# Convolution norms, the sample's softmax, its value pages and half of the even output projection woven into the 32 steps of the prompt attention

## The reference, cut to what matters

```python
z = h @ w_in_even                    # q, k, v, forget gates, a, b
o_fox = fox_attend(q, k, v, logf)    # prompt: causal softmax; sample: 8 pages of 128 keys/values
u = a * sigmoid(b)
cv = depthwise_conv(concat(state, u), width 31) + conv_b
cv = silu(group_norm(cv, 8) * g + b)
out = concat([o_fox, cv]) @ w_out_even     # 512 + 512 features in, 1024 out
x = x + g1 * out
# prompt attention, per head: s = q k^T / 8 + cum_q - cum_k, masked, softmax, p @ v
# sample attention, per sample: the same over cache_k, cache_v[page_table] (1024 rows) and its own row
```

## Time and profile before

| | us |
|---|---|
| median of 3 runs | 1930.45 (1929.25 to 1932.46) |
| profiled execution | 1925.21 |
| its span | 1923.4 |
| TensorE busy / VectorE / ScalarE / GpSimd | 1774.2 / 864.9 / 573.5 / 213.7 |

### The profile page before, as it was taken

How to read it: one execution, slowest core, us unless ns; L and a number is a source line. 1 busy time by engine, 2 the same in 40 slices (tenths; PEclk the granted TensorE clock), 3 DMA queues, 4 the chain that set the end, 5 groups by cost and what they waited for, 6 DMA issues and landing times.

```text
span 1923.4 us, 31960 instructions
## 1 busy us (share of the span) xinstructions
PE 1774.2 (92%) x12929; PEld 1549.1 (81%) x12929; DVE 864.9 (45%) x1461; ACT 573.5 (30%) x816; POOL 213.7 (11%) x229
## 2 busy tenths in 40 slices
PE   5899888779899999999899999999968799999997
PEld 3899443327799999999797879799738799999997
DVE  2699346613533232334634637337463533333324
ACT  2422443201442122122333434314331432222223
POOL 1000048600200000000100101101120100000001
PEclk7899668789999999999999999999978999999998
DMA  8463045577434434443231725334742123233321
GB/s 300 139 214 102 2 138 153 175 256 236 147 94 164 149 103 146 144 139 97 66 105 53 224 76 185 121 91 135 263 141 86 58 88 99 77 97 97 89 72 53
DMA packets 288066, 248.82 MB, mean 129 GB/s; under 512 B 9000, under 2 KB 239816, under 8 KB 287951
## 3 DMA queue, kind: packets, MB, share of 16 engines
q1 hardware_dynamic: 262740, 173.97, 29.8%
q0 software_dynamic: 15824, 58.99, 8.6%
q10 hardware_dynamic: 9395, 14.36, 2.1%
HBM read 224.05 MB, written 23.70 MB: 129 GB/s over the span
## 4 chain that ended last, share of the span: by engine, by line
PE 83%; DVE 6%; ACT 3%; POOL 3%; DMA 2%; issue 2%; ACTq 1%; SPq 0%; POOLq 0%; DVEq 0%
PE product L728 60%; PE product L743 5%; PE job L1140 2%; POOL sqa L2094 2%; DMA vp<-in_cache_v 2%; PE job L625 2%; PE job L619 1%; PE job L1123 1%; PE job L917 1%; PE job L658 1%; PE job L893 1%; PE job L1026 1%; PE job L1115 1%; DVE rstd L1591 1%; PE job L1046 1%
## 5 line engine op out<-in xcount | busy, mean ns | idle before, releaser
L728 PE MATMUL product<-H_hi,w_lo 128*128 128x260 f32 x2368 | 674.1, 285 | 3.0 <-ACT gate L1172 2.9
L728 PE MATMUL product<-H_lo,w_hi 128*128 128x260 f32 x2368 | 668.9, 282 | 0.0
L728 PE MATMUL product<-H_hi,w_hi 128*128 128x260 f32 x2368 | 668.4, 282 | 0.0
L728 PEld LDWEIGHTS product<-H_hi,w_lo 128*128 128x128 f32 x2368 | 445.5, 188 | 16.2 <-issue 14.2
L728 PEld LDWEIGHTS product<-H_hi,w_hi 128*128 128x128 f32 x2368 | 446.1, 188 | 0.0
L728 PEld LDWEIGHTS product<-H_lo,w_hi 128*128 128x128 f32 x2368 | 445.9, 188 | 0.2
L1561 DVE TENSOR_TENSOR w_lo<-raw,w_hi 128x1024 fp32r<-128x1024 f32 (+1 forms) x228 | 274.9, 1207 | 169.1 <-ACT w_hi L1172 168.2
L1172 ACT ACTIVATE w_hi<-raw 128x1024 fp32r<-128x1024 f32 (+1 forms) x228 | 234.6, 1037 | 308.2 <-PE product L728 188.9
L728 PE MATMUL product<-G_hi,w_lo 128*128 128x260 f32 x912 | 260.4, 286 | 5.9 <-DVE X L1645 2.5
L728 PE MATMUL product<-G_lo,w_hi 128*128 128x260 f32 x912 | 259.3, 284 | 0.0
L728 PE MATMUL product<-G_hi,w_hi 128*128 128x260 f32 x912 | 259.2, 284 | 0.0
(11 more groups left out here) (319 smaller groups left out, 2139.3 us busy)
## 6 DMA issues: line engine op xcount, KB each, us to landing
spare<-in_ada_w POOLq DMA_DIRECT2D x24, 1024.0 KB, 9.0
raw<-in_w_in_odd SPq DMA_DIRECT2D x48, 512.0 KB, 3.7
raw<-in_w_ffn_gate SPq DMA_DIRECT2D x44, 512.0 KB, 3.8
raw<-in_w_ffn_up SPq DMA_DIRECT2D x44, 512.0 KB, 3.6
kp<-in_cache_k SPq DMA_DIRECT2D x64, 256.0 KB, 2.7
raw<-in_w_ffn_down SPq DMA_DIRECT2D x32, 512.0 KB, 3.3
st<-in_state_ret POOLq DMA_DIRECT2D x28, 512.0 KB, 4.3
out_ret_sample<-st POOLq DMA_DIRECT2D x28, 512.0 KB, 4.5
```

What stands on the lines that cost most here:

```text
L728: mm = pe.matmul(Gp[slot][:, c, 0:CH], w[:, j, k, :], x[:, k, cols], start=k == 0 and p == 0, stop=k == kt - 1 and p == 2)
```

## The change

Stages 2, 4 and 5 and half of 6 lose their places. Their pieces are put into the steps x of the attention (and a few into the input blocks), each engine's code and the list of PSUM jobs following the same tables:

```diff
+QB_AT = {1: 2, 3: 3, 5: 4, 7: 5, 9: 6, 11: 7}
+VN_AT = {0: (0,), 1: (1,), 2: (2, 3)}
+KN_AT = {6: 0, 8: 1, 10: 2, 12: 3}
+VS_AT, KS_AT, LT_AT, CUM_AT = 4, 14, 3, 5
+CM_AT = {6: 0, 7: 1, 8: 2, 9: 3}
+CQ_AT, ROOT_AT, SILU_AT = 11, 12, 17
+CB_AT = {13: 0, 14: 1, 15: 2, 16: 3}
+PREP_AT = {11: 0, 21: 1}
+MT_AT = {12: 0, 22: 1}
+MB_AT = {13: 0, 23: 1}
+EXP_AT = {14: 0, 24: 1}
+DN_AT = {15: 0, 25: 1}
+V_AT = {17: 0, 19: 1, 21: 2, 23: 3, 27: 4, 29: 5, 31: 6}
+GATHER_AT = {18: 0, 20: 1, 22: 2, 24: 3, 28: 4, 30: 5}
+V_LOAD_AT = {5: (0, 1), 12: (2,), 18: (3, 4), 20: (5, 6), 22: (7, 8), 24: (9, 10), 28: (11, 12), 30: (13, 14)}
+CONV_OUT_AT = {19 + i: i for i in range(8)}
+PER_STEP = 3
+def pages_of(x):
+    return range(min(PER_STEP * x, NPG), min(PER_STEP * x + PER_STEP, NPG))
```

In the input blocks (TensorE; ScalarE and VectorE follow, with the samples' taps at m = 8 to 11 and the log forget values at 10 and 12):

```diff
+                elif m == 9:
+                    conv_rows()
+                elif m == 14:
+                    sums_of_forget()
+                elif m == 15:
+                    rows_of("qs", QT)
+                elif m == 17:
+                    turn_sums()
```

The centring is one product with identity minus mean; ScalarE copies and squares it from PSUM. The group rows are spread by 16 products of half height:

```diff
+            def group_rstd(t):
+                pe.wait_ge(conv_act, 1)
+                for c in range(2):
+                    bank = open_job(("cb", t, c))
+                    for e in range(2):
+                        mm = pe.matmul(bank[HD * e:HD * e + HD, 0:CH],
+                                       con[0:8, C_ID + 2 * t + e:C_ID + 2 * t + e + 1].broadcast_to((8, HD)),
+                                       CR[:, c * CH:(c + 1) * CH], start=True, stop=True)
+                    close(mm)
```

The samples' softmax is made for samples 0 to 3 and 4 to 7 apart. Values go in units of four pages, two units a sample, through three buffers; pages 0 and 1 of a unit are issued by SP, 2 and 3 by ScalarE:

```diff
+        def value_unit(eng, u, js):
+            if u < 2:
+                eng.wait_ge(block_done, N_OUT_EVEN)
+                eng.wait_ge(lo_ready, N_OUT_EVEN)
+            elif u == 2:
+                wait_job(eng, ("cq", 1))
+            elif u % 2 == 0:
+                wait_job(eng, ("ov", (u - 3) // 2))
+            else:
+                eng.wait_ge(v_used, (u - 3) // 2 + 1)
+            for j in js:
+                page(eng, 4 * u + j, cache_v, value_page(u, j), v_unit[u % 3])
...
+            def past_values(b):
+                bank = open_job(("ov", b))
+                pe.wait_ge(samp_dve, 7 + 5 * (b // 4))
+                for u in (2 * b, 2 * b + 1):
+                    pe.wait_ge(v_unit[u % 3], 64 * (u // 3 + 1))
+                    for j in range(4):
+                        mm = pe.matmul(bank[QD * j:QD * j + QD, :], weights_of(b, u % 2 * 4 + j), value_page(u, j),
+                                       start=u % 2 == 0, stop=u % 2 == 1)
+                    if u % 2 == 0:
+                        mm.then_inc(v_used, 1)
+                close(mm)
```

ScalarE copies each sample's bank into vm (before, VectorE multiplied it), and `gather` (`og`) picks the heads by two columns. The output projection becomes 16 blocks of 4 tiles: the convolution's half in steps 19 to 26, with its own update of X, and the attention's half behind the last gather:

```diff
+            def conv_out(i):
+                n = N_OUT_EVEN + i
+                if i == 0:
+                    pe.wait_ge(g_ready, 4)
+                pe.wait_ge(lo_ready, n + 1)
+                slots_free(0, conv_base + i - 1)
+                product(n % 4, n % 2, 4, G_hi[:, 4:8], G_lo[:, 4:8]).then_inc(block_done, 1)
...
+            gather(NB - 2)
+            past_values(NB - 1)
+            gather(NB - 1)
             pe.wait_ge(g_ready, 5)
-            wait_emptied(pe, ("o", HEADS - 1))
-            run("out_even", N_OUT_EVEN, 2, KD, G_hi, G_lo, "D")
+            run("out_even", N_OUT_EVEN + KD, 2, 4, G_hi, G_lo, "D")
```

On ScalarE, four gates, their roundings and two weight splits stand in step 17, and value units in the steps of V_LOAD_AT:

```diff
+                    if x == SILU_AT:
+                        conv_gates()
+                        ahead(N_OUT_EVEN)
+                        ahead(N_OUT_EVEN + 1)
+                    if x in CONV_OUT_AT:
+                        ahead(N_OUT_EVEN + CONV_OUT_AT[x] + 2)
+                    for u in V_LOAD_AT.get(x, ()):
+                        if u == 0:
+                            act.wait_ge(pages_loaded, 32)
+                        value_unit(act, u, (2, 3))
```

On VectorE, behind the dots of a step come the pieces of that step:

```diff
+                    if x == LT_AT + 1:
+                        past_logs()
+                    if x == CUM_AT:
+                        past_sums()
+                    if x in PREP_AT:
+                        past_prepare(PREP_AT[x])
+                    if x == CQ_AT:
+                        group_var()
+                    if x in CB_AT:
+                        group_scale(CB_AT[x])
...
+                    if x == SILU_AT + 1:
+                        for t in range(4):
+                            dve.wait_ge(ghi_ready, t + 1)
+                            n.up(minus_hi(G_lo[:, 4 + t, :], CV[:, t, :], G_hi[:, 4 + t, :]), g_ready)
+                        lo(N_OUT_EVEN)
+                        lo(N_OUT_EVEN + 1)
+                    if x in CONV_OUT_AT:
+                        i = CONV_OUT_AT[x]
+                        lo(N_OUT_EVEN + i + 2)
+                        update(i, N_OUT_EVEN + i, mod_at(0, 2))
```

SP's queue, in order (before: all key pages, four weight blocks, half of the value pages, four weight blocks):

```diff
+            key_pages(0, 4)
+            out_weights(N, N + 4)
+            key_pages(4, 20)
+            values(0, 2)
+            key_pages(20, 36)
+            values(2, 3)
+            key_pages(36, 52)
+            values(3, 5)
+            key_pages(52, 60)
+            values(5, 7)
+            out_weights(N + 4, N + 6)
+            key_pages(60, 64)
+            values(7, 9)
+            out_weights(N + 6, N + 8)
+            values(9, 11)
+            out_weights(N + 8, N + 12)
+            values(11, 16)
+            out_weights(N + 12, N + 16)
```

828 lines of the change are left out of this document (479 added, 349 removed).

## The result

The changed kernel takes 1904.0 us (median of 4 runs, 1900.3 to 1907.5), the kernel before, run beside it, 1930.9: ratio 0.986, interval 0.984 to 0.988. That is 27 us gained where I had forecast 61, and just outside my range. The profiled execution took 1902.9 us with a span of 1901.1.

A forecast was written before the change was run, and what follows sets the result against it. The attention's 32 steps were taken as paced by 64 GpSimd products of 1.27 us, TensorE close behind at clock 0.72. Start 54.5, steps and tail -18, projection 24.5: 61 us gained, profiled 1864, median 1869; range 1840 to 1903.

The forecast's parts named there:

- Start: Stages between input blocks and attention leave the path; GpSimd's first division at 209.3 us, 54.5 earlier.
- Steps 0 to 10: First woven attention steps, three GpSimd products each: GpSimd 47 us, TensorE 48 at full clock, taken as 57 us.
- TensorE needs 28 + 20 = 48 at full clock: In steps 0 to 10, TensorE's products take 48 us if its clock is 1.00.
- Steps 11 to 16: Step 11 with VectorE's 3.4 us reciprocal 11.5 us, the five others 28.5 together: 40 us.
- 17 and 18: Steps with ScalarE's gates, roundings, table loads, weight splits and page issues, and a late key page 52: 18 us.
- the sync queue puts value units ahead of key page 52, some 7 us, beside the same stall: In steps 17 and 18, key page 52 comes some 7 us late, alongside the stall for ScalarE's gates.
- Steps 19 to 26: TensorE's own work, half blocks, values and gathers: 57 us at full clock plus 2 for waits, 59 us.
- Tail: From step 27 until the second projection can start, value pages wait for three buffers: 28.5 us.
- Behind G ready: From the second projection's start to the next norm: half the products and weights' low parts made before, 24.5 us gained.
- the rival that gives 1919: TensorE's clock stays at 0.73 in woven steps and tail, 253 us instead of 202.5; chance 0.10.
- a clock under 0.7 in the woven steps: Sign of being wrong: TensorE's granted clock below 0.7 in the attention steps that carry the added work.
- Queues lock: Rival: four banks shared in one order by all jobs cost 1 us more a step, 32 us, giving 1901; chance 0.20.

The follow-up runs named there:

- split sums: VectorE's seven running additions cut into 2, 3 and 2 over steps 4 to 6, page sums in step 7, against a kernel of 1870.6 us: 1870.5 us.
- the undo: Against keys first, the eight woven half blocks of the convolution's projection run behind the attention instead: 1902.4 us, ratio 0.9859 against 0.9782.
- keys first: Against the changed kernel, the sync queue issues key pages 36 to 63 before the value units they stood behind: 1886.7 us, ratio 0.9782.

## Why the prediction was wrong

The mechanism was the one forecast and its sign was right; five terms of the sum were too small. At the norm the forecast was 437 and the trace has 472.0: 35 us.

*Start*, 209.3 forecast, 213.0 measured (209.5 to 213.4 over all runs). Right to 4 us.

*Steps 0 to 10*, 57 forecast, 61.9 measured, 66 in most other runs. The term is 5 to 10 us too small. The pages aren't the cause (66.8 us without them). The step that failed is "TensorE needs 28 + 20 = 48 at full clock": the attention before had 0.72, and the changed kernel got 0.78 here and has TensorE busy for 55.0 us. In the runs of 66 to 67 us it had 0.68 to 0.73 and was busy for 60 to 63; in the two of 73 and 77 us it had 0.59 and was busy for 70 and 73. The 48 over the clock are 61.5 us at 0.78 and 66 to 71 at 0.73 to 0.68, an estimate from these rows that fits, and 81 at 0.59, which is too much. So the steps lasted about as long as TensorE took at the clock it got. No run changed the clock alone, so this is how the runs go together and not an experiment, and what sets the clock in these steps stays open.

A smaller term was mis-sized too. I took VectorE's seven running additions from a stretch where GpSimd did nothing, 274 ns each. In step 4 GpSimd makes products beside them. The view by tile, of the changed kernel and then of the run with split sums, has their shortest, median and longest:

```profile
L1967 DVE TENSOR_TENSOR EX<-EX,LT x7: 274/275/1222, 240.2 to 243.8; 128x64 f32<-128x64 f32 x7
```

```profile
L1984 DVE TENSOR_TENSOR EX<-EX,LT x7: 266/1224/1232, 242.7 to 256.5; 128x64 f32<-128x64 f32 x7
```

An addition takes 274 ns, or 1.04 to 1.23 us where it meets a product of GpSimd, which takes 1.27. In the change two of the seven met one, and that made them 1.7 us longer (3.85 in all); cut into three pieces six of them did, 7.45 in all. That is 3.6 of the 5.6 us by which steps 0 to 10 are longer there at most, since TensorE's clock fell to 0.59 in the same run. The Trainium skill ("SBUF — State Buffer", Who interferes with whom) has this as a rule: a VectorE instruction with two SBUF inputs contends with a GpSimd instruction that reads SBUF, and the ports that they share are an exclusive lock. Both traces agree with it. I hadn't priced it.

*Steps 11 to 16*, 40 against 47.1, and *17 and 18*, 18 against 21.5. Here the step "the sync queue puts value units ahead of key page 52, some 7 us, beside the same stall" failed, twice over. It isn't beside: with the order mended the steps take 39.7 and 15.6 us. And I had seen one such place where there are three: units 2, 3 and 4, and 5 and 6. The wait before page 36, 9.7 us, had no term at all, although the order was in the diff. Of the 10.5 us by which the two terms were small, the queue's order accounts for all: with it mended the two are 13.3 us shorter. It isn't the clock that gave this in steps 11 to 16, since 6.3 of the 7.4 us there are idle time of TensorE that went (11.1 to 4.8).

The Trainium skill ("ScalarE: Activation LUTs", What ACT_TABLE_LOAD costs) has 2.66 us for a change of set, by which I had the sum 3 to 5 us longer. The trace doesn't bear it out. Step 17 of the changed kernel has a load of 1.28 us, and ScalarE's next instruction begins 0.02 us behind it:

```profile
327.51 1.28 ACT L1317 ACT_TABLE_LOAD   x1
328.81 2.95 ACT L1317 ACTIVATE CV<-CV,vec 128x520 f32<-128x520 f32 x4
```

*Steps 19 to 26*, 59 forecast and 58.7 measured, right by two errors: GpSimd waited 9.3 us in them for page 60, and with the order mended they are 5.1 us shorter; the work itself takes 52 to 54, less than the 57 that I had at the full clock. My term took the half blocks as 23.6 us on top of the rest; the undo shows that they cost these steps 8.3.

*Tail*, 28.5 against 37.9. I had priced the release of a buffer to the landing of its pages at 5.5 to 6 us and counted three waits. That step was too small: two more buffers alone took 8.6 us off, without pages the tail is 25.3, with room for every unit 25.4 to 27.1. I hadn't counted two things that the trace shows. ScalarE issues pages in front of its own copies, 3.7 us in steps 28 and 30 each, and the last unit behind the head's copy; but with two more buffers the tail is 29.3 and 29.5 us with these issues and 29.1 without, so they aren't shown to cost anything there by themselves. And the clock was 0.72, at which the output of the last head took 3.9 us instead of 3.0; in the short tails it is 0.79 to 0.93, and how much of their gain is the clock's isn't separated.

*Behind G ready*, 25.4 against 32.0. "The weights' low parts are made before" and the loads were right; what failed is that I took the norm's own chain as before, hidden below a block of 5.9 us. A block of 2.95 us is shorter than ScalarE's split and square and GpSimd's 1.5 us addition, so the chain came out from under it. Woven in, the stage takes 23.7 to 25.7.

*The clock.* Over the woven steps and the tail it was 0.77 (the stretches above, by their length), near the 0.73 of the rival that gives 1919. I had named a clock under 0.7 in the woven steps as a sign of being wrong, and steps 11 to 18 had 0.65 and 0.66. The rival fails as a whole, for it has TensorE at work all the time, and it was busy for 182 of the 227 us up to G ready; without pages steps 11 to 18 ran at 0.72 and 0.73 and took what I had forecast for a full clock. But it is half right: steps 0 to 10 went with the clock, and steps 11 to 16, with the pages in order, took 45.6 us at 0.61, 41.5 to 42.7 at 0.66 and 39.5 to 39.8 from 0.71 up. In steps 19 to 26 the clock was 0.91. The Trainium skill ("TensorE: Matmul & The Clock Gate", Part 1: The HAM clock gate) has activity release the clock. The trace agrees for the half blocks (0.91 to 0.97), and not for steps 0 to 10, where TensorE is shown busy 55 of 62 us at 0.78 and, with keys first, 0.66 and 0.67 from 200 to 240 us while busy all the time.

*Queues lock*, the rival at 1901, came nearest by its number, and by luck: it meant the four banks that all jobs share, 1 us a step. What locked was the sync queue, in three waits of 9 to 10 us. What the banks cost was not tested.

## What to carry to other kernels

A DMA queue is an in-order engine whose instructions can wait: write down, for each transfer behind a wait, when its consumer needs it, as you would for a compute engine. Key pages ahead of the value units was worth 15 to 17 us, two weights ahead of two units 12 to 15 (by the ratios and by the medians). When a block of work is made shorter, look at what ran beneath it: half the products don't hide the same squares. A term that comes out right as a whole (59 against 58.7) may still be a wait in place of work. And before two profiled executions are compared, look at TensorE's clock in each stretch: the same products took 6 to 11 us more of one stage at a clock lower by 0.1.

The experiments point to a version that beats both kernels: keys first, squares woven, more buffers, and weights before units. Three variants of it take 1867.2 to 1867.8 us, 3.4% below the kernel before and 36 us below the change.

## What the runs showed of the hardware

Page issues whose address is read from the table start 1.1 us apart on their queue, each 0.34 us long (two in 1.44, four in 3.65, eight in 8.05 us), on the sync queue and on ScalarE alike; the two queues issue side by side (two pages each from 407.59 and from 408.73 us in the change). The load on the DMA engines hardly mattered: steps 11 to 26 are 109 us long at 57 to 70% of them busy, and 107 at 0 to 16%. The filler of one product a step went with a clock of 0.93 instead of 0.67 in one stretch, and of 0.52 instead of 0.71 in the next. VectorE's additions of two tiles take 274 ns, or 1.04 to 1.23 us beside a GpSimd product. And eight half blocks in eight steps went with a clock of 0.94 where the same steps without them had 0.65.
